# A two-layer transformer block with mixture of experts on one core: expert steps reordered into small and large in turn, the small step's up product in two parts, scatters shared

## Chip, cores and metric

One core of one Trainium2 chip runs the whole program. The metric is the device time of one execution in microseconds (us); lower is better. All data is float32.

## The reference, cut to what matters

Two layers, each a token mixer and a feed-forward part. Layer 0's feed-forward part is dense, layer 1's is a mixture of experts (`_moe_ffn`) over 256 tokens, 8 experts, 2 experts per token:

```python
logits = h @ w_router                       # 256 x 8
top_val, top_idx = lax.top_k(logits, 2)
gate = softmax(top_val)
# expert e, for the tokens that chose it:
ys = (silu(xs @ w_gate[e]) * (xs @ w_up[e])) @ w_down[e]   # 1024 -> 3584 -> 1024
y = sum over the two experts of gate * ys                  # scatter back to the tokens
x = x + gate_f * y
out = _rmsnorm(x, g_final)
```

The weights of the eight experts are 352 MB, read once from HBM.

## The kernel before

Everything up to about 696 us (both mixers, the dense feed-forward part, the router, the gathering of each expert's tokens into `xall`) is not touched by the change, except for some small VectorE operations at the end of the routing. The change is in the expert part.

**Steps.** An expert's hidden width of 3584 is cut into ES = 4 steps of 896 columns. A step (`step`, L1001) computes gate and up products for its 896 columns, SiLU and the product of the two, turns the hidden tile with TensorE, and adds the down product to banks 4 to 7 of PSUM. Its weights are one job of the stream: 4 pieces of gate (896 KB each), 4 of up (896 KB), 3 of down (1536, 1536, 512 KB), 11.0 MB in all. Each of the three has one buffer only (`eg`, `eu`, `ed`): a piece of the next job can be issued when TensorE has used the same piece of this one (`g_used`, `u_used`, `d_used`). SyncE issues all pieces in one fixed order (L576 to L602): gate, up, down of job 0, then of job 1, and so on, with such a wait ahead of each.

**Classes.** The number of tokens decides how a step is computed (`CAPS`, `UNITS`, L249): class 1 (up to 64 tokens) streams weights against one unit of 64 tokens, on both halves of the array at once (`half`); class 2 (up to 96) adds a `quarter` unit of 32 tokens; class 3 (up to 160) has a `wide` unit of 128 tokens and a quarter; class 4 has two wide ones. The code of each class is in an `If` inside a loop over experts (L1104). By the counts in the trace this input has four experts of class 1, three of class 2 and one of class 3.

**When buffers come free.** In a class 1 step gate and up pieces are freed as they stream. In class 2 and 3 they are freed only by the quarter unit (L951), after the larger unit has gone through gate and up.

**Order.** DVE ranks the experts by class; expert 0 is first, and `TURNS = (0, 1, 7, 2, 6, 3, 5, 4)` puts an expert of class 1 and a larger one in turn: classes 1, 3, 1, 2, 1, 2, 1, 2. All four steps of an expert follow each other.

**Inside a class 1 step**, in TensorE's order: gate 16 products, up 16 products (`hidden`, L930), a wait for DVE's product (`step`, L1524, one operation of 128x512), four transposes into bank 3 (`turn_hidden`, L960), a wait for ScalarE's copies (`turned_hidden`, L1724), 14 down products (L977). Every fp32 product is two MATMUL and two LDWEIGHTS instructions in the trace.

**Ends of experts.** After its four steps an expert's output is copied to `ys` (half by ScalarE, `expert_end` L1771, half by DVE, L1536), TensorE multiplies by the scatter matrix `selgT` (`scatter`, L1084: 4 products for class 1 and 2, 8 for class 3), DVE adds the four results to `yacc` (L1573) and clears banks 4 to 7 (L1511). The next expert's scatter matrix is turned by TensorE (L1075) and copied by ScalarE. After the last expert DVE multiplies `yacc` by the gates (L1578) and adds it to `xs` (L1579); the final norm follows.

**Start of the expert part.** DVE copies the token window of expert 0 (`window(0)`, L1501), then the last gathered tokens, clears banks (L1514), `ys` (L1559) and `yacc` (L1560). TensorE waits ahead of its first gate product for the token window alone (L1105).

## Time and profile before, and how to read them

| | us |
|---|---|
| median of 3 runs | 1682.77 (1682.51 to 1684.44) |
| the profiled execution, its own time | 1683.47 |
| its span, first to last instruction | 1681.7 |
| up to the first gate product | 696.5 |
| the eight experts, first gate to last down product | 696.5 to 1662.1 |
| last scatter, final norm, output | 1662.1 to 1681.7 |
| TensorE busy over the span | 1537.5 (91%) |
| mean granted TensorE clock | 0.970 of 2.4 GHz |

PE is TensorE, PEld its weight loads, DVE is VectorE, ACT ScalarE, SPq SyncE's queue, which issues the transfers. A timeline row has start, duration, engine, line, operation, output<-input, shape and count; in brackets stands the idle time before it and what ended that. "issue" as what ended it means that nothing in the profile released the engine.

### The profile page before, as it was taken

The page shows a single profiled execution, that of the slowest core. Times are in us where ns is not written, and L with a number is a line of the kernel's source. Part 1 is how long each engine was busy: PE and PEld are TensorE (multiplying, and loading weights), DVE is VectorE, ACT ScalarE, POOL GpSimd, SP SyncE. Part 2 cuts the span into 40 slices and gives each one's busy share as a digit, 9 for nine tenths or more (in the row PEclk, how much of TensorE's full clock was granted, in tenths as well). Part 3 has the DMA queues.
Part 4 walks back from the last instruction along what each step waited for, and adds up shares of the span by engine and source line. Part 5 has one row for each costly group of instructions (what it writes and reads, how often), then busy time and mean ns, then how long its engine had stood idle before and what let it go on. Part 6 is the DMA issues. An engine that isn't in the chain of part 4 may idle for free.

```text
span 1681.7 us, 19957 instructions
## 1 busy us (share of the span) xinstructions
PE 1537.5 (91%) x8082; PEld 803.4 (48%) x8083; DVE 416.8 (25%) x892; ACT 268.4 (16%) x589; POOL 0.2 (0%) x4
## 2 busy tenths in 40 slices
PE   5988899999999988897999999899988999988996
PEld 3777558777667873532444433233333333322332
DVE  2366535333235543501000020010110200201004
ACT  2132210000023222211100111111111111111112
POOL 0000000000000000000000000000000000000000
PEclk8999899999999988899999999999999999999998
DMA  9974525665755530399655679999999999999992
GB/s 348 379 260 160 190 100 213 250 250 200 274 201 195 189 137 13 136 408 405 233 195 204 256 286 398 408 407 368 383 401 407 408 395 364 407 408 407 390 382 109
DMA packets 168181, 484.40 MB, mean 288 GB/s; under 512 B 10024, under 2 KB 20544, under 8 KB 168000
## 3 DMA queue, kind: packets, MB, share of 16 engines
q1 hardware_dynamic: 168128, 483.68, 75.6%
q8 instruction: 34, 0.56, 0.1%
q14 instruction: 19, 0.16, 0.0%
HBM read 482.61 MB, written 1.05 MB: 288 GB/s over the span
## 4 chain that ended last, share of the span: by engine, by line
PE 79%; SPq 6%; DVE 6%; DMA 5%; ACT 2%; issue 2%; ACTq 0%; DVEq 0%
PE bank L944 15%; PE bank L993 12%; PE bank L878 9%; PE bank L725 8%; PE bank L955 6%; PE bank L940 6%; PE bank L896 4%; DMA ring<-in_w_exp_up 4%; SPq L592 4%; PE bank L859 4%; PE bank L987 3%; PE bank L719 3%; PE bank L1091 1%; PE bank L974 1%; SPq L598 1%
## 5 line engine op out<-in xcount | busy, mean ns | idle before, releaser
L944 PE MATMUL bank<-ring,hT 128*64 128x448 f32 x1792 | 350.7, 544 | 14.7 <-DMA ring<-in_w_exp_up 12.3
L993 PE MATMUL bank<-ring,bt 128*32 128x256 f32 (+1 forms) x1680 | 244.1, 494 | 18.7 <-ACT bt L1735 16.3
L944 PEld LDWEIGHTS bank<-ring,hT 128*64 128x64 f32 x1792 | 125.0, 137 | 232.2 <-issue 190.6
L1533 DVE TENSOR_TENSOR bt<-arena,bank 128x512 f32<-128x512 f32 (+2 forms) x52 | 35.3, 679 | 787.1 <-PE bank L944 528.1
L993 PEld LDWEIGHTS bank<-ring,bt 128*32 128x32 f32 (+1 forms) x1680 | 75.9, 123 | 173.2 <-issue 109.3
L878 PE MATMUL bank<-hT,ring 128*128 128x256 f32 x704 | 156.7, 383 | 1.7 <-DVE hT L1226 1.7
L725 PE MATMUL bank<-hT,ring 128*128 128x256 f32 x640 | 152.2, 395 | 3.7 <-ACT hT L1620 2.5
L878 PEld LDWEIGHTS bank<-hT,ring 128*128 128x128 f32 x704 | 134.3, 192 | 23.7 <-issue 3.8
L725 PEld LDWEIGHTS bank<-hT,ring 128*128 128x128 f32 x640 | 123.8, 197 | 25.6 <-DVE hT L1226 4.2
L1145 DVE SCALAR_TENSOR_TENSOR acc<-ring,cond,acc 128x512 f32<-128x512 f32 x140 | 105.2, 752 | 4.9
L955 PE MATMUL bank<-ring,hT 128*32 128x448 f32 x1024 | 102.8, 542 | 0.0
L940 PE MATMUL bank<-ring,hT 128*128 128x448 f32 x256 | 99.9, 549 | 0.0
L896 PE MATMUL bank<-ring,arena 128*128 128x512 f32 x176 | 76.6, 593 | 0.0
L940 PEld LDWEIGHTS bank<-ring,hT 128*128 128x128 f32 x256 | 48.6, 192 | 47.6 <-issue 47.6
L1719 ACT ACT_TABLE_LOAD x28 | 35.9, 1283 | 181.1 <-PE bank L944 180.8
L859 PE MATMUL bank<-ring,hT 128*128 128x512 f32 x128 | 59.8, 631 | 1.2 <-DVE hT L1223 1.2
L719 PE MATMUL bank<-ring,hT 128*128 128x256 f32 x256 | 57.1, 381 | 3.1 <-ACT arena L1639 3.1
L955 PEld LDWEIGHTS bank<-ring,hT 128*32 128x32 f32 x1024 | 30.0, 109 | 61.0 <-issue 61.0
L1733 ACT ACTIVATE bt<-bank 64x64 f32<-64x64 f32 (+1 forms) x44 | 9.2, 210 | 285.4 <-PE bank L974 285.4
L719 PEld LDWEIGHTS bank<-ring,hT 128*128 128x128 f32 x256 | 48.1, 190 | 10.8 <-issue 4.5
L987 PE MATMUL bank<-ring,bt 128*128 128x512 f32 x112 | 52.3, 607 | 0.0
L896 PEld LDWEIGHTS bank<-ring,arena 128*128 128x128 f32 x176 | 33.4, 190 | 39.5 <-issue 39.2
(241 smaller groups left out, 964.6 us busy)
## 6 DMA issues: line engine op xcount, KB each, us to landing
ring<-in_w_exp_gate SPq DMA_DIRECT2D x128, 896.0 KB, 8.5
ring<-in_w_exp_up SPq DMA_DIRECT2D x128, 896.0 KB, 14.2
ring<-in_w_exp_down SPq DMA_DIRECT2D x64, 1536.0 KB, 15.4
ring<-in_w_ada SPq DMA_DIRECT2D x24, 2048.0 KB, 9.3
ring<-in_w_in SPq DMA_DIRECT2D x10, 2048.0 KB, 12.9
ring<-in_w_exp_down SPq DMA_DIRECT2D x32, 512.0 KB, 15.6
ring<-in_w_ff_gate SPq DMA_DIRECT2D x5, 2048.0 KB, 12.3
ring<-in_w_ff_up SPq DMA_DIRECT2D x5, 2048.0 KB, 12.7
```

Of the source, the lines that this page charges most:

```text
L592: sp.dma_start(dst[:, 2 * i:2 * i + 2, :], rows_of(w, 2 * i * P, 2 * P, j0, j0 + EW).rearrange("(c p) n -> p c n", p=P))\
L719: last = mm(o[:, b * T:(b + 1) * T], hT[:, k, b * P:(b + 1) * P], w[:, k, :], start=(k == 0), stop=(k == KC - 1))
L725: last = mm(o[:, 0:T], w[:, k, t * P:(t + 1) * P], hT[:, k, :], start=(k == 0), stop=(k == KC - 1))
L859: last = mm(bank[4 + 2 * hf + b][:, :], hT[:, k, b * P:(b + 1) * P], w[:, k, :], start=(k == 0), stop=(k == KC - 1))
L878: last = mm(bank[n % 2][:, a * T:(a + 1) * T], w[a][:, k, t * P:(t + 1) * P], hT[:, k, :], start=(k == 0), stop=(k == KC - 1))
L896: last = mm(bank[4 + 2 * hf + b][:, :], ffT[:, (j - 1) % 2, r, b * P:(b + 1) * P], w[:, r, hf * CW:(hf + 1) * CW], start=(j == 1 and r == ...
L940: last = mm(o[:, 0:EH], xsT[:, k, t0:t0 + P], w[:, k, c * EH:(c + 1) * EH], start=(k == 0), stop=(k == KC - 1))
L944: last = mm(o[64 * c2:64 * c2 + 64, 64 * c2:64 * c2 + EH], xsT[:, k, t0:t0 + 64], w[:, k, c2 * EH:(c2 + 1) * EH], start=(k == 0), stop=(k ...
L955: last = mm(bank[2][32 * q:32 * q + 32, 64 * (q % 2):64 * (q % 2) + EH], xsT[:, k, t0:t0 + 32], w[:, k, (q % 2) * EH:(q % 2 + 1) * EH], st ...
L987: last = mm(bank[4 + 2 * u + hf][:, :], hsT[:, u, t * P:(t + 1) * P], ed[:, t, hf * CW:(hf + 1) * CW], start=False, stop=True, skip_group_ ...
L993: last = mm(bank[4 + 2 * u][m * c:m * c + m, 0:D // parts], hsT[:, u, at_:at_ + m], ed[:, t, c * (D // parts):(c + 1) * (D // parts)], sta ...
L1145: ins = stt(acc[:, :], w[:, k, :], cond[:, k:k + 1], acc[:, :], ALU.mult, ALU.add)
```

## The change

1. The expert order on DVE gets a second table: `STREAM_AT` puts the first small expert, the class 3 expert, small, class 2, small, class 2, small, class 2 at positions 0 to 7, and a flag `misfit` tells whether the classes fit it (expert 0 and the ranks from 5 on of class 1, the largest of class 3 or less). If they do not, the old order runs as an `Else`.
2. If they do, `JOBS` is the order of the 32 jobs. Part l = 0 has 12: for each of the four steps of the class 3 expert one small step ahead of it and one behind it (two small experts in all). Parts l = 1 and 2 have 8 each: small and class 2 step in turn. Part l = 3 is the last class 2 expert alone, 4 steps. SyncE loads in that order.
3. `up_parts`: the small step's up product is two passes over k, of 256 and 192 columns for each half, into banks 1 and 2; DVE multiplies the first part while the second streams; the turn is in two parts too (banks 0 and 3), and so is ScalarE's copy. The small step's output has bank 7, the large one's banks 4 to 6; tokens of small and large steps have their own columns of `xsT`.
4. Scatters: five instead of eight. One after the first small expert (4 products), and one at each part's end for its large and its small expert together (8 products). DVE multiplies each result by the gates and adds it to `yacc`, which starts as a copy of `xs`; the final norm reads `yacc`.
5. TensorE's loops: over l, over i (4 steps), and in it `If`s for the small step, for class 3 or class 2, and for the second small step. Job numbers and counts come from a table (`plan_i`) that each engine reads with `value_load`.

```diff
+STREAM_AT = (0, 1, 3, 5, 7, 2, 4, 6)
+JOBS = []
+for l_ in range(4):
+    for s_ in range(ES):
+        small_ = {0: 2 * (s_ // 2), 1: 4, 2: 6}.get(l_)
+        if l_ != LONE:
+            JOBS.append((small_, 2 * s_ % ES if l_ == 0 else s_))
+        JOBS.append((2 * l_ + 1, s_))
+        if l_ == 0:
+            JOBS.append((small_, 2 * s_ % ES + 1))
...
+            def up_parts(J, ends):
+                for part_, (lo, hi) in enumerate(((0, SPLIT), (SPLIT, EH))):
...
+                        for c2 in range(2):
+                            last = mm(o[64 * c2:64 * c2 + 64, 64 * c2 + lo:64 * c2 + hi], xsT[:, k, TX:T],
+                                      eu[:, k, c2 * EH + lo:c2 * EH + hi], start=(k == 0), stop=(k == KC - 1))
...
+            def turn_parts(J):
+                h = hs[:, 0, :]
+                pe.wait_ge(eh_v, 4 * J + 2)
+                nc.tensor.transpose(bank[0][:, 64:192], h[:, P:2 * P], ident)
+                mm(bank[0][:, 0:64], h[:, 0:P], ident[:, 0:64], start=True, stop=True).then_inc(et_p, 2)
+                pe.wait_ge(eh_v, 4 * J + 4)
+                nc.tensor.transpose(bank[3][:, 192:320], h[:, 2 * P:3 * P], ident)
+                mm(bank[3][:, 320:384], h[:, 3 * P:4 * P], ident[:, 64:P], start=True, stop=True)
+                mm(bank[3][0:64, 384:448], h[:, 3 * P:EH], ident[:, 0:64], start=True, stop=True)
+                mm(bank[3][64:P, 384:448], h[:, 64:P], ident[:, 64:P], start=True, stop=True).then_inc(et_p, 2)
...
+            def small_step(J, ends):
+                pe.wait_ge(xsS_v, ends + 1)
+                pe.wait_ge(yacc_v, 4 * ends + 10)
+                stream_hidden(J, 1, 0, 0, TX)
+                pe.wait_ge(yacc_v, 4 * ends + 11)
+                up_parts(J, ends)
+                pe.wait_ge(yzS_v, ends + 1)
+                turn_parts(J)
...
+            with pe.If(misfit == 0):
+                pe.wait_ge(xsS_v, 1)
+                turn_scatter_weights(0, bank[3])
+                with nc.Fori(0, 4, engines=PE, head_slot={PE[0]: 0}) as l:
+                    which = class_at(pe, 2 * l + 1)
+                    with pe.Fori(0, ES) as i:
+                        J = job_ahead(pe, l, i)
+                        ends = ends_seen(pe, l, i)
+                        with pe.If(l != LONE):
+                            small_step(J, ends)
+                        with pe.If(which == 3):
+                            large_step(l, J + 1, ends, 3)
+                        with pe.Else():
+                            large_step(l, J + 1, ends, 2)
+                        with pe.If(l == 0):
+                            small_step(J + 2, ends)
+                            with pe.If(i == 1):
+                                stream_scatter(0, (1,))
+                    stream_scatter(l + 1, (0, 1))
...
+            with ve.If(misfit == 0):
+                stream_weights(0)
+                gathered(0)
+                small_window(None)
+                gathered(1)
+                large_window(1)
+                ve.wait_ge(sgt_p, 1)
+                stream_weights(1)
+                signal(nc.vector.memset(ys, 0.0), dv)
+                nc.vector.tensor_copy(yacc, xs[:, :, :]).then_inc(yacc_v, 4 * NE + 1 - 20)
+                for i in (4, 5, 6):
+                    last = nc.vector.memset(bank[i][:, :], 0.0)
+                last.then_inc(yzL_v, 1)
...
+                        tt(gated[:, hf, :], bank[2 * b + hf][:, :], gates[:, 1, hf * CW:(hf + 1) * CW], ALU.mult)\
+                            .then_inc(gated_v, 1)
+                        ve.wait_ge(gated_v, 4 * g + n)
+                        y_ = yacc[:, b, hf * CW:(hf + 1) * CW]
+                        tt(y_, y_, gated[:, hf, :], ALU.add).then_inc(yacc_v, 1)
...
-            norm(4, lambda i: ae.wait_ge(x_v, 13 + i // 2))
+            norm(4, lambda i: ae.wait_ge(yacc_v, 4 * NE - 2 + i), yacc)
```

`large_step` (not shown) has the order of the old `step` for class 3 or 2, with bank 3 in place of bank 7 for turns. ScalarE's and DVE's loops follow the same pattern of l, i and `If`.

## Rows read from the trace of the kernel before

**Rows 1.** The page: busy time by engine, and the DMA share in 40 slices.

```profile
PE 1537.5 (91%) x8082; PEld 803.4 (48%) x8083; DVE 416.8 (25%) x892; ACT 268.4 (16%) x589; POOL 0.2 (0%) x4
...
DMA  9974525665755530399655679999999999999992
```

**Rows 2.** Busy time by expert: stretch, length, PE, PEld, DVE, ACT, POOL, clock, DMA, GB/s.

```profile
696.50:791.40 94.90, 84.02 (x393) 29.28 (x392) 12.85 (x17) 15.67 (x26) 0.00 (x0) 0.96 0.99 389
791.40:1001.90 210.50, 204.89 (x925) 91.08 (x924) 15.84 (x26) 23.20 (x49) 0.00 (x0) 0.99 0.63 244
...
1096.80:1221.70 124.90, 122.34 (x891) 42.31 (x888) 13.63 (x23) 19.16 (x41) 0.00 (x0) 1.00 1.00 386
1221.70:1320.60 98.90, 84.42 (x396) 30.20 (x396) 10.01 (x16) 13.45 (x23) 0.00 (x0) 0.97 1.02 404
```

**Rows 3.** TensorE's timeline: one class 1 step and the next one's start.

```profile
1025.54 12.20 PE L944 MATMUL bank<-ring,hT 128*64 128x448 f32 x64
1038.62 0.66 PE L974 MATMUL bank<-ct,bt 128*128 128x128 f32 x4 [0.89 <-DVE bt L1533]
1040.30 6.23 PE L993 MATMUL bank<-ring,bt 128*64 128x512 f32 x28 [1.02 <-ACT bt L1735]
1046.36 0.92 PE L944 MATMUL bank<-ring,hT 128*64 128x448 f32 x4
```

**Rows 4.** The same: a class 3 step, a class 2 step, each to the next one's start.

```profile
895.54 18.31 PE L940 MATMUL bank<-ring,hT 128*128 128x448 f32 x48
...
914.11 0.43 PE L970 MATMUL bank<-ct,bt 128*64 128x128 f32 x2
...
944.44 1.02 PE L940 MATMUL bank<-ring,hT 128*128 128x448 f32 x2
...
1127.94 12.25 PE L944 MATMUL bank<-ring,hT 128*64 128x448 f32 x64
...
1157.43 2.85 PE L944 MATMUL bank<-ring,hT 128*64 128x448 f32 x14
```

**Rows 5.** TensorE's waits from 696 to 1665 us: total, times, longest.

```profile
PE bank L944 <- DMA ring<-in_w_exp_up: 12.3, 24, 0.6
PE bank L1080 <- issue: 8.9, 3, 4.2
```

**Rows 6.** SyncE's line L592 from 1004 to 1017 us: eight gate and up pieces.

```profile
DMA to landing us min/median/max: 4.6/9.1/11.8
```

**Rows 7.** TensorE's timeline at ends of experts, and a slow stretch after one.

```profile
787.72 3.70 PE L1091 MATMUL bank<-arena 128*128 128x512 f32 x8 [0.69 <-ACT arena L1775]
795.67 0.65 PE L1080 MATMUL bank<-ct,arena 128*128 128x128 f32 x4 [4.25 <-issue]
...
994.76 7.13 PE L1091 MATMUL bank<-arena 128*128 128x512 f32 x16 [1.36 <-ACT arena L1781]
1002.61 0.43 PE L1080 MATMUL bank<-ct,arena 128*128 128x128 f32 x2 [0.71 <-issue]
...
1017.78 7.92 PE L993 MATMUL bank<-ring,bt 128*64 128x512 f32 x28 [1.02 <-ACT bt L1735]
```

**Rows 8.** The start of the expert part on TensorE and DVE.

```profile
696.52 12.25 PE L944 MATMUL bank<-ring,hT 128*64 128x448 f32 x64
...
697.68 2.11 DVE L1514 MEMSET bank<- 128x512 f32 x4 [2.00 <-ACT ring L1706]
...
702.35 1.76 DVE L1560 MEMSET arena<- 128x2048 f32 x1 [0.37 <-issue]
```

**Rows 9.** DVE and ScalarE: a window copy, the last addition to `yacc`, the norm.

```profile
1208.62 1.23 DVE L1501 COPY hT<-ring 128x2048 f32 x1 [1.11 <-issue]
...
1667.32 0.69 DVE L1573 TENSOR_TENSOR arena<-arena,bank 128x512 f32<-128x512 f32 x1 [0.17 <-PE bank L1091]
...
1672.70 0.63 ACT L1600 ACTIVATE xn<-xs 128x512 f32<-128x512 f32 x1 [7.66 <-DVE xs L1579]
...
1677.32 1.28 DVE L1586 SCALAR_TENSOR_TENSOR xn<-xs,st,bt 128x1024 f32<-128x1024 f32 x1
```

More of the change, by code:

```diff
@@ new lines, in small_down @@
+            def small_down(J, tiles):
+                for t in tiles:
+                    if t in (0, 3, 6):
+                        pe.wait_ge(full_d[t // 3], 16 * J + 16)
+                    at_ = PARTS_AT[t] * 64
+                    for c in range(2):
+                        last = mm(bank[7][64 * c:64 * c + 64, 0:CW], hsT[:, 0, at_:at_ + 64],
+                                  ed[:, t, c * CW:(c + 1) * CW], start=False, stop=True, skip_group_check=True)
+                    if t in (2, 5, 6):
+                        last.then_inc(d_used, 1)
@@ L1576, in _, with small_window, large_window @@
-            ve.wait_ge(yacc_v, 4 * NE + 1)
-            for b in range(2):
-                then(tt(yacc[:, b, :], yacc[:, b, :], gates[:, 1, :], ALU.mult))
-                signal(tt(xs[:, b, :], xs[:, b, :], yacc[:, b, :], ALU.add), x_v)
-            own(x_v)
+            def small_window(pos):
+                t0 = start_of(ve, expert_at(ve, pos, NE)) if pos is not None else 0
+                nc.vector.tensor_copy(xsT[:, :, TX:T], xall[:, :, bass.ds(t0, T - TX)]).then_inc(xsS_v, 1)
+            def large_window(pos):
+                t0 = start_of(ve, expert_at(ve, pos, NE))
+                nc.vector.tensor_copy(xsT[:, :, 0:CAPS[2]], xall[:, :, bass.ds(t0, CAPS[2])]).then_inc(xsL_v, 1)
@@ new lines, in stream_weights @@
+            def stream_weights(g):
+                large = None if isinstance(g, int) and g == 0 else expert_at(ve, 2 * g - 1, NE)
+                small = 0 if large is None else expert_at(ve, 2 * g, NE)
+                for b in range(2):
+                    dst = selg[:, b, 0:TX]
+                    if large is None:
+                        nc.vector.memset(dst, 0.0)
+                    else:
+                        ts(dst, slots[:, 0:TX], pos[:, b, bass.ds(large, 1)], gate[:, b, bass.ds(large, 1)],
+                           ALU.is_equal, ALU.mult)
+                    last = ts(selg[:, b, TX:T], slots[:, 0:T - TX], pos[:, b, bass.ds(small, 1)],
+                              gate[:, b, bass.ds(small, 1)], ALU.is_equal, ALU.mult)
+                last.then_inc(selg_v, 1)
@@ new lines, in _ @@
+            counted, count = count, counted
+            with ve.Else():
+                scatter_weights(0)
+                gathered(0)
+                window(0)
+                gathered(1)
+                clear_banks()
+                signal(nc.vector.memset(ys, 0.0), dv)
+                signal(nc.vector.tensor_copy(yacc, xs[:, :, :]), yacc_v)
+                with ve.Fori(0, NE) as r:
+                    which = class_of(ve, r)
+                    for n in range(1, 5):
+                        with ve.If(which == n):
+                            with ve.Fori(0, ES) as s:
+                                step(r * ES + s, n)
+                            expert_end(r, n)
+                    ve.wait_ge(yacc_v, 4 * r + 1)
+                    for b in range(2):
+                        for hf in range(2):
+                            ve.wait_ge(sct_p, 4 * r + 2 * b + hf + 1)
+                            tt(gated[:, hf, :], bank[(2, 6)[hf] + b][:, :], gates[:, 1, hf * CW:(hf + 1) * CW], ALU.mult)\
+                                .then_inc(gated_v, 1)
+                            ve.wait_ge(gated_v, 4 * r + 2 * b + hf + 1)
+                            y_ = yacc[:, b, hf * CW:(hf + 1) * CW]
+                            tt(y_, y_, gated[:, hf, :], ALU.add).then_inc(yacc_v, 1)
+                    ve.wait_ge(yacc_v, 4 * r + 5)
+                    clear_banks()
@@ L1798 @@
+            with ae.Else():
+                with ae.Fori(0, NE) as r:
+                    which = class_of(ae, r)
+                    for n in range(1, 5):
+                        with ae.If(which == n):
+                            scatter_matrix(r, n)
+                            with ae.Fori(0, ES) as s:
+                                step(r * ES + s, n)
+                            expert_end(r, n)
+            norm(4, lambda i: ae.wait_ge(yacc_v, 4 * NE - 2 + i), yacc)
 def kernel(**inputs):
```

352 lines of the change are left out of this document (288 added, 64 removed).

## The prediction, as put on record before the result

> **What bounds the kernel now.** I read the busy row and the slices of the page first: TensorE is busy 91% of the span, and in the last 23 slices, the expert part, the transfers are near 100% too, except in five slices at five to seven tenths [rows 1]. Two resources, each near its limit: the question is which one ends last in each stretch. The table by expert answers it [rows 2]. A class 1 expert has TensorE busy 84 of 95 or 99 us with the transfers at 0.99 to 1.02; the class 3 expert has TensorE busy 205 of 210.5 us with the transfers at 0.63; a class 2 expert has both full (122 of 125 us, 1.00). So only one long stretch leaves the transfers idle, and there TensorE works at its own pace.
>
> The unit prices come from TensorE's timeline. A class 1 step takes 1046.36 - 1025.54 = 20.82 us: 12.20 of gate and up, 0.66 of turn, 6.23 of down, and waits of 0.89 (for DVE) and 1.02 (for ScalarE) [rows 3]. A class 3 step takes 944.44 - 895.54 = 48.90, a class 2 step 1157.43 - 1127.94 = 29.49 [rows 4]. A job is 11.01 MB; at the 404 GB/s of the fullest stretch [rows 2] it takes 27.2 us, and as a few of that stretch's microseconds still had room I take 27.1.
>
> TensorE's own sum: 16 x 20.82 + 12 x 29.49 + 4 x 48.90 = 882.6 us, of 965.6 us between the first gate product (696.5) and the last down product (1662.1). The other 83 us are: seven ends of experts, each a copy wait of 0.7 to 1.4, a scatter of 3.70 (7.13 for class 3) and a turn of 0.4, and three waits that end by "issue" with 8.9 us together [rows 5, 7], 47 us in all; stretches at the low level of the clock, 1.2 of 2.4 GHz, as the down products that took 7.92 where 6.23 is usual [rows 3, 7], the shown one by 1.7 and some six in all by the mean clock of 0.96 to 0.99 [rows 2], 10 us; the remaining 26 are waits for weights and what surrounds them, of which the table names 12.3 for up pieces [rows 5]. This is the point to see: **weights cost TensorE only some 26 us in all**, so no order of the steps can give more than that, and TensorE's work is not less in the new order.
>
> **The small step.** Up in two parts has 32 products in place of 16, with 256 and 192 columns: by columns the same 6.02 us. The trace has no stream of 192 columns over 64 rows. Bounds: 0, and +0.8 if each of the 16 passes of the short part takes as long as one of 256 columns would (0.215 by 12.20 / 32 / 448 x 256, instead of 0.16). I take +0.3, nearer to the columns, as the trace's streams go by them. Then the turn: first part 0.6 (one transpose at 0.16 [rows 3], one product against the identity at 0.43 [rows 4]), which now runs while DVE does the second part (two operations of 192 columns: 0.26 each by columns from 0.69 for 512 [rows 9], 0.69 at most, I take 0.36); second part 1.2; ScalarE's first copy lies beside it, its second beside three down tiles. From the end of up to the first down product 2.2 instead of 2.57. Net 20.7, bounds 20.3 to 21.3. The split nearly pays for itself and gives nothing more: the wait of 1.02 for ScalarE goes, but four more identity products come.
>
> **Waits for weights in the new order.** A small step lags the transfers by 27.1 - 20.7 = 6.4 us, a class 2 step gives 2.4 back, so a pair lags 4.0. How much lag is free? Pieces land 4.6 us after their issue when the queue is empty, the eighth one 11.8 after its issue at 1015.3 [rows 6], that is 24.1 after the small step's start at 1003.0. A large step behind it asks for its last up piece 20.7 + 6.0 + 4.5 = 31.2 after that start: 7.1 us of slack. Four pairs lag 16; 16 - 7.1 = 9 us of waits in each of l = 1 and 2, and I take 8.4, since the first pair starts with pieces in hand. The slack is small because the large step frees gate and up only in its quarter unit; four small steps in a row had more. In l = 0 a round (small, large, small: 90.3 us) is longer than its three transfers (81.3), so TensorE sets the pace; only two small steps in a row ahead of a large one wait, 2 us twice.
>
> **Ends.** After the first small expert 5.0 (0.7 + 3.7 + 0.65 [rows 3, 7]). At a part's end the copies of a large output (a wait of 1.36) and of a small one (0.69) follow each other: 2.0; 8 products take 7.13 [rows 7], the turn 0.65: 9.8, three times before the last part. DVE's two operations per result (1.4 us) keep up with 1.8 per result. The gate stream waits for the first addition alone, which is done 2.6 us into a scatter: covered.
>
> **A new wait at the start.** This is the term that I think is easiest to miss. `small_step` waits for `yacc_v` >= 10, and the first increments come with DVE's copy of `xs` to `yacc`. Before, TensorE started at 696.52 while DVE cleared `ys` and `yacc` until 704.1 [rows 8]. Now DVE has ahead of that copy, from 697.6: two register reads (1.1, the idle before a window copy [rows 9]), a window of 1280 columns (0.8 by 1.23 for 2048 [rows 9]), reads and four mask operations (1.6), clearing `ys` with its start gap (2.1), and the copy (1.4): 704.9. TensorE's first gate product moves from 696.5 to 705.0, **+8.5**, and the transfers, already full for job 0, wait with it. Bounds +6 to +10.
>
> **Tail.** From last down to the end 19.6 before. Now 2.0 + 7.1 of scatter, DVE's two operations to 10.9; ScalarE first copies the (unused) next scatter matrix, then loads its square root table and does the norm (4.4, from 1672.70 to shortly before 1677.32): 16.0; DVE also clears banks and makes two unused masks before it scales (1.28): 18.2; output 1681.7 - 1678.6 = 3.1 [rows 9]: 21.3, **+1.7** (bounds -2 and +4).
>
> **Code.** Each jump over the other class's body needs code that may not be near. Before, the first end of a class 1 expert shows 4.25 us ended by "issue" after a 3.70 scatter, and class 3's end 0.71 after 7.13 [rows 7]: in both cases some 7.9 us from the scatter's start. The waits by "issue" are three, 8.9 us in all [rows 5]; the other ends have none, and the loops' own jumps back over a whole step have none [rows 4]. I take the first few far jumps as such waits, 6 us in sum.
>
> **The sum.** l = 0: 4 x 48.9 + 8 x 20.7 + 5 + 4 = 370.2. l = 1, 2: 2 x (4 x 50.2 + 8.4) = 418.4. l = 3: 118.0. Ends 29.4. Together 936.0. Start 8.5, low clock 4 (the middle gap that brought most of it is shorter), code 6, register reads ahead of SyncE's issues 1, unexplained as before 2: 957.5, against 965.6: -8.1. With the tail -6.4. The profiled execution took 1683.47; that makes 1677.1, and 0.7 less against the median of 1682.77. I say **1677**. The gain is three scatters saved and fewer "issue" waits; half of it goes back at the start.
>
> **Rivals.**
> B, faster: code is in place after its first use, the clock stays at its high level, waits for weights are halved: 6 + 2 + 5 less, 1664. For it: only three of seven ends had the wait [rows 5].
> C, slower: **far jumps fetch each time.** The place is TensorE's queue at each boundary between step bodies, 27 of them (7 in l = 0, 16 in l = 1 and 2, 4 in l = 3). Price: 7.9 us less the 4 to 6 us of products still queued, 2.5 each: 67 us, less the 21 us of waits for weights that it hides: +46, 1722. It decides above 1 us per boundary. Against it: four of the seven ends before, which jump between bodies too, have no such wait [rows 5]. The Trainium skill ("Runtime: NRT & Kernel Launch", Instruction fetch mechanics) says that prefetch is sequential only and that a taken branch outside the resident blocks stalls for a fetch; by that rule every one of these boundaries would stall, and the free ends of the trace speak against it in that form.
> D, slower: the small step comes out at 21.3 and register reads show by 0.5 in 20 iterations: 5 + 8 more, 1690. It decides in l = 0, where TensorE sets the pace.
> E, the change does not do what it says: the classes do not fit the flag and the old order runs, with gates multiplied per result: 1684. The counts of forms (one class 3, three class 2, expert 0 class 1) speak against it.
>
> **How the numbers follow.** A measurement of this kernel tells about 0.2% (3.4 us) from no change. Forecast 0.47, of which 0.36 below 1679.4 and 0.11 in the band; its own range is 1670 to 1686. B 0.15, all faster. C 0.13, all slower. D 0.17, of which 0.04 in the band. E 0.08, of which 0.07 in the band. Faster 0.51, same 0.22, slower 0.27. The range 1662 to 1698 takes in A, B, D and E with the bounds of their terms and leaves most of C out.
>
> **What would show it.** First gate product near 705, with DVE's copy as releaser; small steps near 20.7; four waits for up pieces in the last two pairs of l = 1 and 2, about 3.8 each; ends of 9.8; last down near 1654. Wrong: "issue" waits at most boundaries (C), a first gate product near 697 (the start term), or classes 1, 3, 1, 2 in blocks of four steps (E).

## The result, and the profile after

The changed kernel takes 1672.12 us (median), the kernel before 1683.6 beside it: ratio 0.993, 95% interval 0.992 to 0.994. Measured again beside the last experiments it was 1670.15 against 1683.72, ratio 0.993 (0.991 to 0.994). One of its first five executions took 4051 us, in a slow state, and the ratio leaves it out. The forecast was 1677, so the direction and the range hold, and the gain is nearly twice the one forecast.

The page of the changed kernel, busy row and transfers in 40 slices (compare [rows 1]):

```profile
PE 1544.0 (92%) x8696; PEld 852.4 (51%) x8697; DVE 418.1 (25%) x955; ACT 250.2 (15%) x560; POOL 0.2 (0%) x4
...
DMA  9974525765656440068979797999999999997991
```

Busy time by part of the changed kernel: part 0, 1 and 2, each with its end, then part 3 to the end of the program (stretch, length, PE, PEld, DVE, ACT, POOL, clock, DMA, GB/s):

```profile
708.30:1087.70 379.40, 366.41 (x2009) 169.06 (x2009) 36.33 (x76) 38.72 (x78) 0.00 (x0) 1.00 0.88 342
1087.70:1307.20 219.50, 206.44 (x1438) 82.36 (x1437) 22.77 (x47) 29.06 (x57) 0.00 (x0) 1.00 1.01 401
1307.20:1528.40 221.20, 208.19 (x1437) 82.91 (x1436) 22.76 (x47) 29.05 (x57) 0.00 (x0) 0.99 1.02 401
1528.40:1670.40 142.00, 125.81 (x901) 45.03 (x900) 24.07 (x44) 24.38 (x56) 0.00 (x0) 0.97 0.67 257
```

Read against [rows 2]: the one stretch that left the transfers idle (class 3, 0.63) is now spread over part 0 at 0.88, and parts 1 and 2 have them full with their ends. TensorE's waits from 700 to 1672 us (compare [rows 5]):

```profile
PE bank L1024 <- DMA ring<-in_w_exp_up: 12.7, 24, 0.6
PE bank L1280 <- ACT arena L2162: 8.9, 5, 2.1
PE bank L1024 <- DVE arena L1866: 8.1, 1, 8.1
PE bank L1024 <- issue: 7.1, 10, 3.2
PE bank L1199 <- DVE bt L1801: 6.2, 16, 0.4
PE bank L1024 <- DMA ring<-in_w_exp_gate: 4.3, 8, 0.6
PE bank L1020 <- DMA ring<-in_w_exp_up: 3.4, 7, 0.6
```

The third row is the new wait at the start, 8.1 us at once. TensorE's timeline shows it, and then one small step to the next step's start (compare [rows 3]):

```profile
699.60 0.60 PE L1269 MATMUL bank<-ct,arena 128*128 128x128 f32 x4
708.30 4.07 PE L1024 MATMUL bank<-ring,hT 128*64 128x448 f32 x12 [8.11 <-DVE arena L1866]
...
985.49 6.18 PE L1024 MATMUL bank<-ring,hT 128*64 128x448 f32 x32
991.50 6.22 PE L1185 MATMUL bank<-ring,hT 128*64 128x256 f32 x64
997.65 0.33 PE L1196 MATMUL bank<-ct,bt 128*128 128x128 f32 x1
...
998.54 0.33 PE L1199 MATMUL bank<-ct,bt 128*128 128x128 f32 x1 [0.39 <-DVE bt L1801]
...
999.13 6.18 PE L1211 MATMUL bank<-ring,bt 128*64 128x512 f32 x28
1005.24 3.27 PE L1020 MATMUL bank<-ring,hT 128*128 128x448 f32 x8
```

And the end of part 0, scatter and turn (compare [rows 7]):

```profile
1080.20 7.13 PE L1280 MATMUL bank<-arena 128*128 128x512 f32 x16 [1.94 <-ACT arena L2162]
1087.17 0.60 PE L1269 MATMUL bank<-ct,arena 128*128 128x128 f32 x4
```

The small step takes 1005.24 - 985.49 = 19.7 where the old one took 20.8. Up in two parts (32 products, 64 instructions) takes 6.22 by this row, against half of 12.20 in one stream [rows 3], so the split itself is nearly free; from the end of up (997.7) to the first down product are 1.4 us, one short wait of 0.39 in them, in place of 2.57 with two waits.

| us, profiled executions | before | forecast | changed |
|---|---|---|---|
| up to the first gate product | 696.5 | 705.0 | 708.3 |
| first gate to last down product | 965.6 | 949.0 | 940.5 |
| last down product to the end of the span | 19.6 | 21.3 | 21.6 |
| its own time | 1683.47 | 1677.1 | 1672.14 |

### The profile page after: what moved, and what is told of

It is laid out like the page before. It is cut to its first block, busy times and chain, and to the rows that moved or that the text cites. A ratio compares the mean times of both kernels' runs of the same rounds, so it can differ in the third digit from the quotient of the medians.

```text
span 1670.4 us, 21757 instructions
## 1 busy us (share of the span) xinstructions
PE 1544.0 (92%) x8696; PEld 852.4 (51%) x8697; DVE 418.1 (25%) x955; ACT 250.2 (15%) x560; POOL 0.2 (0%) x4
## 4 chain that ended last, share of the span: by engine, by line
PE 79%; DMA 9%; DVE 5%; SPq 3%; ACT 2%; issue 2%; DVEq 0%; ACTq 0%
PE bank L1024 11%; PE bank L931 9%; PE bank L1064 8%; DMA ring<-in_w_exp_up 8%; PE bank L778 7%; PE bank L1008 6%; PE bank L1185 6%; PE bank L1020 5%; PE bank L949 4%; PE bank L912 4%; PE bank L1058 3%; PE bank L1211 3%; PE bank L772 3%; SPq L629 2%; PE bank L1280 2%
## 5 line engine op out<-in xcount | busy, mean ns | idle before, releaser
L1024 PE MATMUL bank<-ring,hT 128*64 128x448 f32 x1280 | 255.1, 546 | 32.2 <-DMA ring<-in_w_exp_up 12.7
L1024 PEld LDWEIGHTS bank<-ring,hT 128*64 128x64 f32 x1280 | 89.0, 137 | 190.7 <-issue 153.7
L1809 DVE TENSOR_TENSOR bt<-arena,bank 64x512 f32<-64x512 f32 (+2 forms) x36 | 24.3, 675 | 493.5 <-PE bank L1024 249.6
L1064 PE MATMUL bank<-ring,bt 128*32 128x256 f32 (+1 forms) x1232 | 136.8, 445 | 0.0
L1185 PE MATMUL bank<-ring,hT 128*64 128x192 f32 (+1 forms) x1024 | 99.6, 352 | 0.0
L1211 PE MATMUL bank<-ring,bt 128*64 128x512 f32 x448 | 98.9, 592 | 0.0
L1064 PEld LDWEIGHTS bank<-ring,bt 128*32 128x32 f32 (+1 forms) x1232 | 44.0, 116 | 89.4 <-issue 52.2
L1185 PEld LDWEIGHTS bank<-ring,hT 128*64 128x64 f32 x1024 | 74.6, 137 | 29.1 <-issue 7.4
L1020 PEld LDWEIGHTS bank<-ring,hT 128*128 128x128 f32 x256 | 47.1, 190 | 55.8 <-issue 46.4
L1796 DVE TENSOR_TENSOR bt<-arena,bank 128x256 f32<-128x256 f32 x16 | 6.7, 422 | 274.7 <-PE bank L1185 274.7
L1211 PEld LDWEIGHTS bank<-ring,bt 128*64 128x64 f32 x448 | 30.5, 137 | 55.2 <-issue 52.0
## 6 DMA issues: line engine op xcount, KB each, us to landing
ring<-in_w_in SPq DMA_DIRECT2D x10, 2048.0 KB, 12.8
ring<-in_w_exp_down SPq DMA_DIRECT2D x32, 512.0 KB, 16.3
ring<-in_w_ff_up SPq DMA_DIRECT2D x5, 2048.0 KB, 12.8
```

The costliest lines, as they stand in the source:

```text
L1020: last = mm(o[:, 0:EH], xsT[:, k, t0:t0 + P], w[:, k, c * EH:(c + 1) * EH], start=(k == 0), stop=(k == KC - 1))
L1024: last = mm(o[64 * c2:64 * c2 + 64, 64 * c2:64 * c2 + EH], xsT[:, k, t0:t0 + 64], w[:, k, c2 * EH:(c2 + 1) * EH], start=(k == 0), stop=(k ...
L1064: last = mm(bank[first_bank + 2 * u][m * c:m * c + m, 0:D // parts], hsT[:, u, at_:at_ + m], ed[:, t, c * (D // parts):(c + 1) * (D // par ...
L1185: last = mm(o[64 * c2:64 * c2 + 64, 64 * c2 + lo:64 * c2 + hi], xsT[:, k, TX:T], eu[:, k, c2 * EH + lo:c2 * EH + hi], start=(k == 0), stop ...
L1211: last = mm(bank[7][64 * c:64 * c + 64, 0:CW], hsT[:, 0, at_:at_ + 64], ed[:, t, c * CW:(c + 1) * CW], start=False, stop=True, skip_group_ ...
```

## The experiments

All ratios are against the kernel before on the same chip; 0.1% there is 1.7 us. The letters name the theory and the rivals of each expectation. "Low level" is the lower of TensorE's two granted clocks, 1.2 of 2.4 GHz; how many us a stretch spent there is added up from the clock record of its trace.

**The start wait.** In the changed kernel:

```diff
                 small_window(None)
+                nc.vector.tensor_copy(yacc, xs[:, :, :]).then_inc(yacc_v, 4 * NE + 1 - 20)
                 gathered(1)
...
                 signal(nc.vector.memset(ys, 0.0), dv)
-                nc.vector.tensor_copy(yacc, xs[:, :, :]).then_inc(yacc_v, 4 * NE + 1 - 20)
```

> The changed kernel, with DVE's copy of xs to yacc (and its signal) moved ahead of the second half of the gathered tokens; nothing else. Theory T (TensorE sets the pace from the first gate product to the end of part 0, so a wait at its start passes through whole): the first gate product is not at 708.3 but near 700.3, some 8 us earlier, and the time falls by 8, from 1672.1 to 1664; with the low clock stretch at 704.7, if the idle time ahead of it brought it, 1662.5. Rival S (the transfers set the pace from job 1 on, and make up for a late start while TensorE is idle): the first gate product moves all the same, the time by less than 3, 1669 to 1672. DVE's copies of gathered tokens come 0.5 to 1 us later, which by neither shows.

Measured 1662.11, ratio 0.9873 (0.9858 to 0.9889). Its trace has the copy on VectorE at 694.15, and TensorE's first gate product right behind the gathering:

```profile
697.16 0.60 PE L1269 MATMUL bank<-ct,arena 128*128 128x128 f32 x4
697.98 2.48 PE L1024 MATMUL bank<-ring,hT 128*64 128x448 f32 x12 [0.22 <-issue]
```

T holds: the whole wait passes through to the end. The ratios are 0.58% apart, some 9.8 us, which by the two intervals is known to some 3 us; 7.9 are the wait (8.11 less 0.22), and 1.6 that the first 16 gate products took 7.8 behind it, at the low clock, and take 6.2 here. One moved copy nearly doubles what the change gives.

**The small step in the new order.** In the changed kernel, the small step of before:

```diff
-                up_parts(J, ends)
+                pe.wait_ge(yacc_v, 4 * ends + 12)
+                stream_hidden(J, 1, 0, 1, TX)
                 pe.wait_ge(yzS_v, ends + 1)
-                turn_parts(J)
-                pe.wait_ge(et_a, 4 * J + 2)
-                small_down(J, range(0, 2))
-                small_down(J, range(3, 4))
+                turn_hidden(J, 1, 0, "half", bank[3])
                 pe.wait_ge(et_a, 4 * J + 4)
-                small_down(J, (2, 4, 5, 6))
+                small_down(J, ALL)
```

(with VectorE's one product and ScalarE's copies as before)

> The changed kernel with the small step as before the change (one stream for up, one product by VectorE, four transposes, one wait for ScalarE); order and scatters stay. The small step is then 20.8 us again, where the changed kernel's trace has 19.7. Theory T (part 0 at TensorE's pace, parts 1 and 2 at that of the transfers, whose share there is 1.01 to 1.03): the 1.1 us count in the eight small steps of part 0 and not in the eight of parts 1 and 2: +9, 1681. Rival P (TensorE's steps count everywhere): 16 x 1.1 = +18, 1690. Rival F (the forecast's reckoning, where the split gave 0.1 a step): +1 to +2, 1673.5.

Measured 1685.76, ratio 1.0009 (0.9996 to 1.0022), 13 us above the changed kernel: between T and P, far from F. Its table by part:

```profile
703.29:1097.46 394.17, 373.17 (x1705) 150.83 (x1705) 31.11 (x52) 40.34 (x86) 0.00 (x0) 0.97 0.85 334
1097.46:1319.82 222.36, 205.93 (x1285) 72.24 (x1284) 20.12 (x35) 29.86 (x61) 0.00 (x0) 0.99 0.99 387
1319.82:1540.66 220.84, 205.50 (x1285) 72.39 (x1284) 20.13 (x35) 29.86 (x61) 0.00 (x0) 0.99 1.01 399
```

Parts 1 and 2 are 2.9 longer and 0.4 shorter, 2.5 together and not 8.8 (8 steps of 1.1), which is T. Part 0 is 14.8 longer, not 8.8, which is not T: its clock is 0.97 where the changed kernel has 1.00. The clock record has 37 us at the low level between 699 and 1660 here, 10 in the changed kernel, 20 in the kernel before. The parts come to 17 us more, and the executions of the two profiles are only 12 apart, because this one reached its first gate product 5.0 earlier (703.29, 708.30), for a reason ahead of the expert part (see the start, below).

**What brings the low clock.** In that kernel TensorE gets work of no use in the two waits of each small step:

```diff
+            def fill(n):
+                for _ in range(n):
+                    mm(bank[2][:, 0:P], ident, ident, start=True, stop=True)
...
                 stream_hidden(J, 1, 0, 1, TX)
+                fill(5)
                 pe.wait_ge(yzS_v, ends + 1)
                 turn_hidden(J, 1, 0, "half", bank[3])
+                fill(6)
                 pe.wait_ge(et_a, 4 * J + 4)
```

> The kernel with up as one stream in the new order (12 us slower than the changed one by its profile), and in each small step's two waits, for VectorE and for ScalarE, TensorE multiplies the identity by itself, 5 and 6 times, into an unused bank: about the 0.9 and 1.0 us of the waits, so that no step is shorter. That kernel has nine stretches of low clock in the expert part after its start, the changed one has one. Theory U (the idle time of some 1.9 us in each small step brings the low clock, 3.4 us at half speed, 1.7 lost each): with the waits filled one or two of the nine are left and the time falls by 6 to 12 against that kernel, ratio to before 0.994 to 0.997, though the fill takes nothing out of any step. Rival V (the stretches come from something else, or cost nothing): the same as without the fill, 1.0009, or above it by what the fill overshoots (16 x 0.2).

Measured 1681.5, ratio 0.999 (0.9979 to 1.0): 3 to 4 below the kernel without the fill, less than U said, and with intervals that overlap a little, so the time alone gives no verdict. The clock does: in the 11 executions that the ratio without the fill rests on its mean is 0.962 to 0.969, 0.965 on average, and in the 12 with the fill 0.968 to 0.974, 0.972 on average. The timeline says why the time gained less: the fill is too long, so that the step takes 1114.28 - 1092.95 = 21.3 and not 20.8, 4 us in part 0:

```profile
1092.95 12.25 PE L1024 MATMUL bank<-ring,hT 128*64 128x448 f32 x64
1105.13 1.38 PE L1219 MATMUL bank<-ct 128*128 128x128 f32 x10
1106.35 0.60 PE L1045 MATMUL bank<-ct,bt 128*128 128x128 f32 x4
1106.78 1.50 PE L1219 MATMUL bank<-ct 128*128 128x128 f32 x12
1108.22 6.23 PE L1211 MATMUL bank<-ring,bt 128*64 128x512 f32 x28
1114.28 12.20 PE L1024 MATMUL bank<-ring,hT 128*64 128x448 f32 x64
```

and part 0 still is shorter:

```profile
703.00:1092.95 389.95, 383.70 (x1880) 168.97 (x1881) 31.09 (x52) 40.34 (x86) 0.00 (x0) 0.99 0.86 337
```

389.95 against 394.17, with steps that are longer by 8 x 0.5: 8 us came back with the clock, which goes from 0.97 to 0.99; the low level is down from 37 us to 17. V is out. The idle time inside the small step cost twice, once by itself and once in the clock behind it, and the split in two parts, which leaves 0.39 of it, takes most of both away. These waits do not settle the clock by themselves, though: the kernel before has the same two in all 16 class 1 steps, and 20 us at the low level where the new order with them has 37. Why the order matters for it is not shown.

**The new small step in the old order.** In the kernel before, `up_parts`, `turn_parts`, VectorE's four operations and ScalarE's two copies of the change, and nothing else:

> The kernel before (old order, eight scatters) with the new small step alone. Theory T (class 1 experts run at the pace of the transfers, 0.98 to 1.03, so a shorter step waits for weights): the 16 x 1.1 us are hidden, and at most the low clock stretches that its waits brought go, -1 to -5, ratio 0.997 to 1.0. Rival P (the step's saving counts wherever it stands): -15 or more, 0.991.

Measured 1685.84, ratio 1.0013 (1.0004 to 1.0022): P is out, and T holds for the step itself; but the 1 to 5 us that T gave to the clock are not there, and the 2 us above the kernel before have no cause shown. A class 1 expert is at the pace of the transfers, so the time saved comes back as waits for up pieces, here in the third step of the first expert:

```profile
740.18 1.03 PE L1014 MATMUL bank<-ring,hT 128*64 128x256 f32 x8
742.11 1.08 PE L1014 MATMUL bank<-ring,hT 128*64 128x256 f32 x8 [0.89 <-DMA ring<-in_w_exp_up]
744.36 1.08 PE L1014 MATMUL bank<-ring,hT 128*64 128x256 f32 x8 [1.17 <-DMA ring<-in_w_exp_up]
746.62 5.37 PE L1014 MATMUL bank<-ring,hT 128*64 128x256 f32 x40 [1.17 <-DMA ring<-in_w_exp_up]
```

The table's waits for up pieces are 23.7 us, where the kernel before has 12.3 [rows 5]. They are idle time as well: this profile has 41 us at the low level. But it is of one of the slower executions (1688.26), and over all 11 the mean clock is 0.969, against 0.967 before, so the clock does not explain the result. So neither half of the change gains alone: the new order (with its shared scatters and its start wait) with the old step 1.001, the old order with the new step 1.001, both 0.993. The first of these carries the start wait, which by the experiment above costs about 0.6%; an estimate from the two is 0.995 for the new order with the old step and no start wait, which was not run.

**The rest of the program.** The changed kernel with `rank > 1.5` made `rank > 0.5` in the first term of `misfit`, so that the old order always runs:

> The changed kernel with its flag always set to misfit: the same program takes the old order, the old small step and eight scatters; only the gates are multiplied per result (as in the changed kernel) and the norm reads yacc. Theory T: nothing of the gain is left, the first gate product is near 700 (the start wait is in the other branch alone), 1683 to 1685; the last gates' multiply and addition saved at the end about make up for one product more per result. Rival (part of the gain comes from elsewhere in the program, code placement or the shorter end): 1677 or less.

Measured 1686.18, ratio 1.002 (1.001 to 1.003): nothing of the gain is elsewhere. It lies 1 us above T's range. Its waits by "issue" are four with 13.8 us (three with 8.9 before); the added one, 4.65, stands ahead of its first gate product (700.62), and it covers the 3 us.

**What each order leaves for the transfers to cost.** Both kernels with half of each piece (`EW // 2` columns of gate and up, `D // 2` of down are loaded; the products run over the whole buffer, so the results are of other numbers):

> The changed kernel; of every expert's piece of gate, up and down weights only half of the columns is loaded (the other half holds old data, so products are on other numbers). It shows TensorE's own time in the new order. Theory T: parts 1 and 2 fall from 209.9 to 4 x 49.2 = 197 each, part 0 by its waits for weights, 5 to 8; the whole by 31 to 34, to 1638 to 1641. Rival P (waits for weights cost little, as the table's 21 us for pieces say): 1651. Part 3 stays at 120.4 by both, since its waits end by nothing that the profile shows.

> The kernel before; of every expert's piece of gate, up and down weights only half of the columns is loaded. Beside the same edit of the changed kernel (36.6 us below it) it shows what each order leaves for the transfers to cost. Theory T (the new order waits more for weights, and has less work of its own): 26 to 28 less than the kernel before, 1655 to 1657, so that TensorE's own time is 20 us shorter in the new order (16 steps by 1.1, scatters, fewer stretches of low clock, less the 8 of the start), and 8 to 10 of these are given back to waits for weights. Rival O (the alternation gains by overlapping transfers better): the kernel before falls by more than the changed one, by 40 or more, to 1643 or less. TensorE's stretches of low clock stay as they are in both, or nearly.

Measured 1635.5 (0.9718) and 1655.27 (0.983): 36.6 below the changed kernel by its first median, 34.7 by its second, and 28.0 below the kernel before, from two executions each. T in the second; in the first it said 31 to 34, and the fall is a little larger; P (1651) and O (1643) are out. TensorE's own time is 20 us shorter in the new order although it starts 8 later, and some 7 to 9 of it go to waits for weights. By part the changed kernel loses 9.2 in part 0 (of which 2.7 are a wait by "issue" that falls from 3.17 to 0.52) and 12.2 in each of parts 1 and 2:

```profile
704.46:1074.66 370.20, 363.93 (x2008) 169.80 (x2008) 36.35 (x76) 38.72 (x78) 0.00 (x0) 1.00 0.55 179
1074.66:1282.01 207.35, 202.81 (x1437) 83.93 (x1436) 22.78 (x47) 29.05 (x57) 0.00 (x0) 1.00 0.65 213
1282.01:1491.06 209.05, 204.51 (x1438) 84.51 (x1437) 22.79 (x47) 29.06 (x57) 0.00 (x0) 0.99 0.63 211
```

**Blocks in parts 1 and 2.** In the changed kernel, the steps of these parts small x 4, then large x 4:

```diff
 for l_ in (1, 2):
+    JOBS += [(2 * l_ + 2, s_) for s_ in range(ES)] + [(2 * l_ + 1, s_) for s_ in range(ES)]
...
                         with pe.If(l == 0):
                             large_step(l, J + 1, ends, 3)
                             small_step(J + 2, ends)
...
+                    with pe.If(l != 0):
+                        jobs = first_large(pe, l)
+                        with pe.Fori(0, ES) as i:
+                            large_step(l, jobs + i, ends_seen(pe, l, i), 2)
```

> The changed kernel with blocks in parts 1 and 2: the four steps of the small expert, then the four of the class 2 expert, in TensorE's order and in that of the loads; part 0, part 3, the ends and the scatters stay. In the changed kernel the transfers are at 1.01 to 1.03 through parts 1 and 2 and their ends. Theory T (the queue is the pace there, in either order; four large steps in a row let it stand still for some 2 us each): +3 to +6, 1675 to 1678. Rival O (alternation is what gained): the small block waits 7.4 a step and the large block gives nothing back, +13 or more, 1685 and up. Rival N: within 1.5 of the changed kernel.

Measured 1682.57, ratio 0.9997 (0.9984 to 1.0009), 11 to 12 above the changed kernel: by the total, near rival O (13 or more). The trace divides it otherwise. Parts 1 and 2 take 223.4 and 224.0 in place of 219.5 and 221.2, 6.7 together, of which part is clock (0.98):

```profile
1084.20:1307.60 223.40, 210.19 (x1437) 83.85 (x1436) 22.72 (x47) 30.32 (x58) 0.00 (x0) 0.98 1.01 396
1307.60:1531.60 224.00, 209.55 (x1437) 82.75 (x1436) 22.85 (x47) 30.32 (x58) 0.00 (x0) 0.98 1.01 396
```

and part 3, whose steps are the same, takes 6.5 more, most of it one wait ahead of its loop:

```profile
1531.04 0.60 PE L1270 MATMUL bank<-ct,arena 128*128 128x128 f32 x4
1536.91 3.93 PE L1025 MATMUL bank<-ring,hT 128*64 128x448 f32 x10 [5.28 <-issue]
```

So the alternation in parts 1 and 2 is worth about 7 us, a little over T's 3 to 6, and the rest is this edit's own wait of 5.28 and the low clock behind it (0.93 in part 3, 0.97 in the changed kernel). In part 3 this kernel first runs four rounds of the loop over i that hold no step, only table reads and branches; whether they take the 5.28 or a fetch of code does is not divided. The body behind the wait had been used in parts 1 and 2 already.

**Longer ends.** In the changed kernel, at the ends of parts 0 and 1:

```diff
+                    with pe.If(l != LONE):
+                        with pe.If(l != 2):
+                            for _ in range(43):
+                                mm(bank[2][:, 0:P], ident, ident, start=True, stop=True)
                     stream_scatter(l + 1, (0, 1))
```

> The changed kernel with 43 products of the identity with itself (7 us at 0.16 each, 2 of them in place of the wait for the copies) ahead of the scatter at the ends of parts 0 and 1, so that TensorE's end takes some 5 us more, twice: about what a scatter and turn of its own would cost. Theory T (through parts 1 and 2 the transfers are the pace, and go on through the ends at 1.02): the 10 us are hidden, +0 to +3, so sharing the scatters of these parts gave nothing. Rival E (ends lie on TensorE's path): +10, 1682.

Measured 1682.95, ratio 1.0 (0.9991 to 1.0009), 12.8 above the changed kernel on this chip. The fill takes 9.7, not 7, and replaces a wait of 2.0, so an end is 7.7 longer. Twice that is 15.4, and with 1.7 less for a low stretch that is gone some 13.7 are expected if an end counts whole. Nearly all of it is there: E, and T falls on this point. The table shows an end of part 0 in its two halves:

```profile
1074.10:1083.80 9.70, 9.70 (x89) 9.70 (x88) 3.48 (x6) 1.82 (x4) 0.00 (x0) 1.00 1.03 409
1083.80:1091.20 7.40, 7.40 (x24) 3.36 (x22) 4.49 (x7) 0.00 (x0) 0.00 (x0) 1.00 0.73 293
```

The queue is full for the first half and then runs out: SyncE issues the last down piece at 1074.3 and nothing until 1093.1, when the next step begins to free its gate pieces. With one buffer per piece the transfers can be one job ahead and no more. Through an end of 9.6 us they have enough left to do (1.02); the 7.7 us over that count whole. What a shorter end in part 0, 1 or 2 would give was not tried. A share of 1.0 over a stretch does not say that TensorE's time in it is free.

**A short end, and part 3 in a loop of its own.** With yacc copied first:

```diff
-                    stream_scatter(l + 1, (0, 1))
+                    with pe.If(l != LONE):
+                        stream_scatter(l + 1, (0, 1))
+                last_scatter()
...
+                        mm(bank[2 * b + hf][:, :], selgT[:, 0, b * P:(b + 1) * P], ys[:, 0, hf * CW:(hf + 1) * CW],
+                           start=True, stop=True).then_inc(sct_p, 1)
```

> The changed kernel with yacc copied first (1662.1, 9 to 10 below the changed kernel), and a last end of its own: the lone class 2 expert's output is scattered with 4 products in place of 8 (the second tile of ys is the small expert's, and no one reads its result there), without the copies of bank 7, the next scatter matrix, the cleared banks and the masks; a class 3 expert in the last place counts as a misfit. From the last down product to the end the changed kernel takes 21.6: 2.1 of wait, 8.6 to the last addition, then a copy of an unused matrix and the table load ahead of the norm. Theory: wait 1.4, last addition 6.5 after the first product, the norm's first half beside the additions, 14.7 in all: -6 to -7, 1655.5. Rival: the transfer of the output and the norm's chain set the end and only the scatter's own 3.5 go: 1658.6.

Measured 1655.63, ratio 0.9839 (0.9821 to 0.9856), 6.5 below the kernel with yacc first, as the theory said. The interval takes in the rival's 1658.6 too, so the trace has to divide them, and it gives the end less than the theory did: from the last down product to the end of the span it takes 16.3 where the changed kernel takes 21.6, 5.3 less, and the theory had 14.7. ScalarE now loads its table (1.28) while TensorE scatters, and its norm runs beside VectorE's additions; the scatter is 3.70 long:

```profile
1636.31 1.28 ACT L1950 ACT_TABLE_LOAD   x1
1636.34 3.70 PE L1291 MATMUL bank<-arena 128*128 128x512 f32 x8 [1.48 <-ACT arena L2170]
```

Then part 3 apart:

```diff
-                with nc.Fori(0, 4, engines=PE, head_slot={PE[0]: 0}) as l:
+                with nc.Fori(0, LONE, engines=PE, head_slot={PE[0]: 0}) as l:
...
+                with pe.Fori(0, ES) as i:
+                    large_step(LONE, i + 28, 4, 2)
                 last_scatter()
```

> The kernel with yacc first and the short end (1655.6), with the lone class 2 expert's four steps in a loop of their own, without the table reads and the branches on part and class. Its steps take 30.3 us in the changed kernel, 29.5 in the kernel before, with 0.7 that nothing in the profile releases ahead of each. Theory R (TensorE's sequencer reads registers and takes branches there, and its queue runs dry at a step's end): 0.7 goes three times, part 3 is 118.2, -2: 1653.5. Rival G (the 0.7 belongs to the jump back over the body, as a fetch): the same as with the common loop, or slower by a first fetch of the new body, 3 to 5.

Measured 1653.63, ratio 0.9829 (0.9816 to 0.9842). R: the step starts without a wait at 1546.55 and the next at 1576.03, 29.5 apart as in the kernel before, where the changed kernel has 30.2:

```profile
1588.99 12.25 PE L1024 MATMUL bank<-ring,hT 128*64 128x448 f32 x64 [0.73 <-issue]
...
1619.21 0.97 PE L1024 MATMUL bank<-ring,hT 128*64 128x448 f32 x4 [0.66 <-issue]
```

(changed kernel). Whether the table reads or the branches take the 0.7 is not divided. The two medians are 2.0 apart, as expected, but their intervals overlap, so that the trace carries this verdict. This version is 1.7% faster than the kernel before, and 1.0% faster than the changed one.

**The changed kernel again**, beside these:

> The changed kernel itself, beside the others on their chip: ratio to the kernel before 0.993, 1672, by every theory.

Measured 1670.15, ratio 0.9926 (0.9913 to 0.9939).

## Why the prediction was right, and where its terms were off

The path was right, and in part 0 and in parts 1 and 2 the number came close by errors that cancel.

**The small step is the term that was mis-sized.** The prediction put it at "Net 20.7, bounds 20.3 to 21.3" and said that "the split nearly pays for itself and gives nothing more". It measured 19.7, outside the bounds. Of the terms, the split cost about 0.1 to 0.2 in place of 0.3, and from the end of up to the first down product the parts took 1.4 in place of 2.2: the short identity products of both turn parts together take about 1.1, VectorE's second part is waited for by 0.39 only, and no copy of ScalarE is waited for. The forecast added up durations of short products from their rows (0.43 for one against the identity), and in the trace such products overlap: the rows of 0.33 start 0.16 to 0.27 apart. In part 0 that is 8 us, more than the whole miss against the profiled execution (1677.1 - 1672.14 = 5.0). The full effect of the step is larger than its length, by the low clock that the old waits brought. That was in the forecast's low clock term (10 to 4), but put down to a shorter gap in the middle, not to the small step's waits.

**The start was right.** Forecast +8.5, shown 8.11 with VectorE's copy as releaser, and 7.9 taken away by one moved line. The first gate product came at 708.3 and not at 705.0 because the gathering's products began 3.1 later (683.77, and 680.69 before), behind work that the change does not touch: TensorE had 20 us at the low clock level near 186 us, 10 in the kernel before. That belongs to the execution and not to the kernel: in the second profile of the changed kernel it had 14 us there, and the gathering began at 681.29 and the first gate product came at 705.65. From the start of the gathering to the first gate product it is 24.5 in the changed kernel and 15.8 before, 8.7 more. The terms of the forecast for VectorE add up to 704.6, not to the 704.9 it has, which changes nothing.

**Part 0** was 370.2 in the forecast and is 370.0 up to the last down product, by errors that cancel: 8 less for the small steps; 3.2 for a fetch and 1.6 for the low clock at its start, which the forecast had in terms of their own; and 2.3 and 4.2 of waits for weights where two small steps precede the large one, 6.5 for 4.

**Parts 1 and 2** were 418.4 and are 419.8, again by two errors: TensorE's own work is 8 less, and the waits are 13 a part where 8.4 were taken. Here a shorter step only waits longer.

**Ends** of 9.8 are 9.4, 9.6 and 11.3, the last one in a stretch of low clock (8.83 for 7.13 of scatter). **Low clock** of 4 is 3.3: 6.8 us at the start and 3.4 at that end. Of the first only 3.2 lie behind the first gate product, and half of those and of the 3.4 is lost. **The tail** of 21.3 is 21.6, with the copy of an unused matrix and the table load in it as described.

**Code.** The forecast took 6 us; the changed kernel has one wait of 3.17, ahead of the second small step of part 0 at its first use, and the later far jumps have none or 0.3 to 0.7. Rival C is out: some 27 boundaries, and one long wait:

```profile
781.85 6.23 PE L1024 MATMUL bank<-ring,hT 128*64 128x448 f32 x32 [3.17 <-issue]
```

The Trainium skill ("Runtime: NRT & Kernel Launch", Instruction fetch mechanics) has every taken branch outside the resident blocks stall. In this trace no boundary stalls like that again: the same one has no wait in its later rounds, and the class 2 body, first used at 1107.4, had none. The wait of 3.17 is gone in the kernel with blocks, where part 0 has no class 2 body to jump over, and it is 0.52 in the kernel with half of the weights. That fits a fetch of code behind queued transfers, but no row shows the fetch itself. It also cost next to nothing: part 0 with its end takes 379.4 in the kernel with blocks too, since its next steps then wait for weights (0.4 to 0.7 for a piece from 811 on).

**What was missed:** 0.7 us ahead of three steps of part 3, 120.4 for 118.0. Rival D had such a term, 0.5 in 20 iterations; it shows in nine, with 3.9 us: six times 0.3 in parts 1 and 2, where the transfers set the pace, and three times 0.7 in part 3, where it counts. Its price for rival D is also off: 0.5 in 20 iterations is 10, and it put 8.

Summed from the first gate to the last down product:

| us | forecast | measured |
|---|---|---|
| part 0 | 370.2 | 370.0 |
| parts 1 and 2 | 418.4 | 419.8 |
| part 3 | 118.0 | 120.4 |
| three ends | 29.4 | 30.3 |
| apart: low clock 4, code 6, register reads 1, unexplained 2 | 13.0 | within the rows above (3.2 fetch, 3.3 clock) |
| sum | 949.0 | 940.5 |

So the mechanism of the order was right: fewer scatters, and no "issue" waits at these ends. Seven ends took 47.2 before (last down product to the next gate product: 9.1, 9.6, 4.5, 9.6, 4.5, 5.3, 4.5), four take 35.0 now (4.7, 9.4, 9.6, 11.3). What it did not see is that the small step's gain needs the new order, and that the new order, with its start wait, gains nothing without it, which the two kernels with one half of the change each show.

What stays open: how much of the low clock a single wait of 0.4 to 1 us brings. The fill was tried in both waits together only, and the kernel before, with the same waits, has less of it. It is open too why the new small step in the old order comes out 2 us above the kernel before.

## What to carry to other kernels

A saving inside a step counts only where that step's engine sets the pace. Here the same 1.1 us a step were worth nothing with the small steps in blocks and about 13 us with the large ones between them, so measure a local change together with the order that exposes it. A transfer share of 1.0 does not make the other engine's ends free when the buffers hold one job: here the queue was full through an end of 9.6 us and ran out in one of 17.1. And look for what the first wait of a stage now hangs on: one copy placed behind clearing and masks cost 8 us, some two thirds of what the change brought.

## What the runs showed of the hardware that was not expected

- **Short idle gaps on TensorE can bring the low clock.** In the new order with two waits of 0.9 and 1.0 us in each small step, 37 us of the expert part were at the low level; with useless products in the same waits 17, and 8 us of part 0 came back although every step was 0.5 longer. In the old order the same waits went with 20 us.
- **Register reads and branches of a loop can show between two rounds of it**: 0.7 us a step with a table read and three branches, none in a plain loop over the same body.
- **A product of the identity with itself is not priced like a transpose.** 43 of them took 9.7 us, 0.225 each, in two instructions; a transpose of the same 128x128 is one instruction at 0.16. The expectations of both fills took the one for the other, and their steps and ends came out longer than meant.
